# One table and one 8 KB gather for both expert vectors, in tiles of 64 tokens by 2 heads

## What is computed

```python
v1, i1 = lax.top_k(s1, TOPK_HALF)          # 128 key scores per half, the best 16
v2, i2 = lax.top_k(s2, TOPK_HALF)
cand_s = v1[..., :, None] + v2[..., None, :]   # 256 candidates per head
top_s, pos = lax.top_k(cand_s, TOPK)           # the best 16
gate = jax.nn.softmax(top_s, axis=-1)
u = expert_u[it]                               # (tokens, 8, 16, 1024)
vv = expert_v[it]
act = jax.nn.gelu(jnp.einsum('thkd,td->thk', u, xt), approximate=False)
return jnp.einsum('thk,thkd->td', gt * act, vv)
```

## Time and profile before

| | us |
|---|---|
| median of 3 runs | 3206.51 (3203.05 to 3211.17) |
| span of the profiled execution | 3215.5 |
| TensorE busy | 2267.0 (71%) |
| VectorE busy | 2051.6 (64%) |
| ScalarE busy | 296.6 (9%) |
| GpSimd busy | 2249.6 (70%) |
| moved | 1210.54 MB, mean 376 GB/s |

### The profile page before, as it was taken

How to read it: one execution, slowest core, us unless ns; L and a number is a source line. 1 busy time by engine, 2 the same in 40 slices (tenths; PEclk the granted TensorE clock), 3 DMA queues, 4 the chain that set the end, 5 groups by cost and what they waited for, 6 DMA issues and landing times.

```text
span 3215.5 us, 27380 instructions
## 1 busy us (share of the span) xinstructions
PE 2267.0 (71%) x9248; PEld 950.2 (30%) x9248; DVE 2051.6 (64%) x4962; ACT 296.6 (9%) x476; POOL 2249.6 (70%) x2062
## 2 busy tenths in 40 slices
PE   7877568878666588777765578887767665556666
PEld 5553323423233134223322224432322221111111
DVE  2588865666777855655788855666587776444441
ACT  1120001110000011111000000122000000000000
POOL 0246666787777776777777776778777777777775
PEclk9878779889778799989877788889988887787668
DMA  5799999999999999999999999999999999999998
GB/s 198 280 344 363 375 359 409 409 342 410 379 367 378 367 410 409 400 352 377 409 394 382 382 372 409 383 360 346 384 402 382 406 376 384 408 408 406 409 410 321
DMA packets 332348, 1210.54 MB, mean 376 GB/s; under 512 B 37040, under 2 KB 37168, under 8 KB 332208
## 3 DMA queue, kind: packets, MB, share of 16 engines
q0 software_dynamic: 294912, 1073.87, 86.5%
q1 hardware_dynamic: 37296, 134.91, 11.0%
HBM read 1204.44 MB, written 4.19 MB: 376 GB/s over the span
## 4 chain that ended last, share of the span: by engine, by line
POOL 35%; issue 12%; DVE 10%; DMA 7%; PE 6%; ACT 0%; POOLq 0%; DVEq 0%
POOL v_ring L436 18%; POOL u_ring L424 17%; DMA v_ring<-table_v,idx_v 5%; DVE u_ring L998 4%; DMA u_ring<-table_u,idx_u 3%; PE acc L632 2%; PE pt L462 2%; PE po L462 1%; DVE rc L867 1%; DVE rc L872 1%; DVE top_i L818 0%; DVE top_i L828 0%; DVE top_v L825 0%; DVE top_v L815 0%; DVE sum_p L853 0%
## 5 line engine op out<-in xcount | busy, mean ns | idle before, releaser
L998 DVE CUSTOM_DVE_ANT_0 u_ring<-u_ring,h2s 128x1024 f32<-128x1024 f32 x1024 | 1238.6, 1223 | 884.1 <-DMA u_ring<-table_u,idx_u 870.6
L632 PE MATMUL acc<-v_ring,wmask 128*32 128x512 f32 x4096 | 1229.4, 765 | 558.4 <-DMA v_ring<-table_v,idx_v 512.7
L424 POOL DMA_INDIRECT u_ring<-table_u,idx_u x1024 | 1115.4, 1089 | 604.5 <-issue 297.8
L436 POOL DMA_INDIRECT v_ring<-table_v,idx_v x1024 | 1130.5, 1104 | 349.4 <-issue 303.4
L632 PEld LDWEIGHTS acc<-v_ring,wmask 128*32 128x32 f32 x4096 | 220.7, 126 | 1435.9 <-DMA v_ring<-table_v,idx_v 1144.2
L462 PE MATMUL pt<-hT,w_ring 128*128 128x256 f32 (+1 forms) x1440 | 276.9, 350 | 10.5 <-DVE uT L911 9.9
L462 PEld LDWEIGHTS pt<-hT,w_ring 128*128 128x128 f32 x1440 | 237.1, 199 | 56.3 <-issue 32.8
L462 PE MATMUL po<-hT,w_ring 128*128 128x256 f32 (+1 forms) x800 | 158.2, 353 | 9.6 <-ACT kT L692 7.7
L462 PEld LDWEIGHTS po<-hT,w_ring 128*128 128x128 f32 x800 | 132.2, 198 | 38.7 <-issue 25.1
L618 PE MATMUL small<-ident,idx_f 128*32 128x32 f32 x256 | 13.5, 242 | 157.6 <-DVE idx_u L881 150.3
L451 PE MATMUL pt<-ident,rb 128*128 128x128 f32 x284 | 48.1, 321 | 68.2 <-ACT rb L667 42.2
(11 more groups left out here) (160 smaller groups left out, 1669.6 us busy)
## 6 DMA issues: line engine op xcount, KB each, us to landing
w_ring<-wstream SPq DMA_DIRECT2D x240, 512.0 KB, 6.8
u_ring<-table_u,idx_u POOLq DMA_INDIRECT x1024, 7.9
v_ring<-table_v,idx_v POOLq DMA_INDIRECT x1024, 7.9
xs<-x_in_dram SPq DMA_DIRECT2D x8, 512.0 KB, 8.3
y_out_dram<-xs SPq DMA_DIRECT2D x8, 512.0 KB, 6.6
g_all<-norm SPq DMA_DIRECT2D x1, 512.0 KB, 8.2
keysT<-keys SPq DMA_DIRECT2D x1, 128.0 KB, 7.2
chan_sb<-chan SPq DMA_DIRECT2D x1, 19.0 KB, 7.8
```

What stands on the lines that cost most here:

```text
L424: nc.gpsimd.indirect_dma_start(out=u_ring[:, k % U_SLOTS, :], out_offset=None, in_=peer_u, in_offset=bass.IndirectOffsetOnAxis(ap=idx_u[:, ...
L436: nc.gpsimd.indirect_dma_start(out=v_ring[:, slot, :], out_offset=None, in_=peer_v, in_offset=bass.IndirectOffsetOnAxis(ap=idx_v[:, b % ST ...
L632: mm = nc.tensor.matmul(acc[32 * i:32 * i + 32, half * 512:(half + 1) * 512], wmask[:, quarter % 2, i, 32 * j:32 * j + 32], v_ring[:, t % ...
L998: d = V.tensor_tensor_reduce(u, u, h2s[:, b % STASH, :], 1.0, 0.0, ALU.mult, ALU.add, dots[:, quarter % 2, at:at + 1])
```

## The change

The two tables become one, `table_uv`, with 2048 columns: a row holds an expert's U row and behind it its V row, so one gather of 128 rows of 8 KB (1 MB) brings both. For this the U and the V side must share one tile: tile `t` holds 64 tokens (half `t % 2` of a block) times the two heads of a quarter, at one pick rank. One ring of 8 slots of 8 KB replaces two rings of 8 slots of 4 KB. The diff, cut to its core:

```diff
-        u_ring = sb("u_ring", [P, U_SLOTS, D])
-        v_ring = sb("v_ring", [P, V_SLOTS, D])
+        ring = sb("ring", [P, SLOTS, 2 * D])
...
+        def place(t):
+            b, q, r, i = t // PICKS, t % PICKS // QPICKS, t % QPICKS // 2, t % 2
+            return b, q, i, r
...
-            for s in range(BLOCKS * GROUPS + V_LAG):
-                if s >= V_LAG:
-                    gather_v(s - V_LAG)
-                if s < BLOCKS * GROUPS:
-                    gather_u(s)
+            for t in range(TICKS):
+                b, q, i, r = place(t)
+                if t % QPICKS == 0:
+                    pool.wait_ge(idx_kept, picked(b, q))
+                if t % 2 == 0:
+                    wait(pool, pair_done, (t - SLOTS) // 2 + 1)
+                nc.gpsimd.indirect_dma_start(
+                    out=ring[:, t % SLOTS, :], out_offset=None, in_=table,
+                    in_offset=bass.IndirectOffsetOnAxis(ap=idx_t[:, b % STASH, q, i, r:r + 1], axis=0),
+                ).then_inc(uv_in[t % SLOTS], 16)
...
+            def mix(p):
+                if p % PAIRS == 0:
+                    wait(pe, acc_free, p // PAIRS)
+                pe.wait_ge(wmask_ready, p + 1)
+                for half in range(2):
+                    for i in range(2):
+                        slot = (2 * p + i) % SLOTS
+                        mm = nc.tensor.matmul(acc[HALF * i:HALF * i + HALF, half * 512:(half + 1) * 512],
+                                              wmask[:, slot, :],
+                                              ring[:, slot, D + half * 512:D + (half + 1) * 512],
+                                              start=(p % PAIRS == 0), stop=(p % PAIRS == PAIRS - 1))
+                mm.then_inc(pair_done, 1)
...
+                if k % 2 == 0 and 0 < k <= TICKS:
+                    mix(k // 2 - 1)
                 for step in STEPS.get(k, ()):
...
+            def gate_mask(p):
+                for t in (2 * p, 2 * p + 1):
+                    b, q, i, r = place(t)
+                    a = nc.scalar.activation(gmask[:, t % SLOTS, :], stack[:], copy,
+                                             scale=gate_t[:, b % STASH, q, i, r:r + 1])
+                a.then_inc(gmask_ready, 1)
+            def weigh(p):
+                lo = 2 * p % SLOTS
+                act.wait_ge(dots_done, p + 1)
+                nc.scalar.activation(acts[:, lo:lo + 2], dots[:, lo:lo + 2], ACT.Gelu).then_inc(gelu_done, 1)
+                act.wait_ge(gmask_ready, p + 1)
+                act.wait_ge(gelu_done, p + 1)
+                for slot in (lo, lo + 1):
+                    a = nc.scalar.activation(wmask[:, slot, :], gmask[:, slot, :], copy,
+                                             scale=acts[:, slot:slot + 1])
+                a.then_inc(wmask_ready, 1)
```

```diff
-        (566, 748, 780, 812, 844)]
+        (584, 744, 776, 808, 840)]
```

More of the change, by code:

```diff
@@ L125, in front_steps, with peer, ranks @@
     main += [(2.0, ("h2", b)) for b in blocks]
+    def peer(p):
+        return [(piece, ("w", PIECE_PEER + 4 * p + c)) for c in range(4)] + [(3.0, ("key_scores", p))]
+    def ranks(b, q):
+        return [(7.0, ("rank", b, q)), (5.5, ("combine", b, q)), (0.5, ("gate", b, q)),
+                (6.5, ("look_up", b, q)), (1.5, ("turn_picks", b, q))]
+    if f == 0:
+        first = ranks(0, 0)
+        main += peer(0) + first[:2] + peer(1) + peer(2) + first[2:4] + peer(3)[:2] + first[4:] + peer(3)[2:]
+        return [main] + [ranks(0, q) for q in range(1, 4)]
     sections = [main, [], [], []]
     for q, section in enumerate(sections):
-        for p in (range(0) if f == 0 and q else range(4) if f == 0 else (q,)):
-            main_or_own = main if f == 0 else section
-            main_or_own += [(piece, ("w", PIECE_PEER + 4 * p + c)) for c in range(4)]
-            main_or_own += [(3.0, ("key_scores", p))]
+        section += peer(q)
         for b in blocks:
-            section += [(9.0, ("rank", b, q)), (7.0, ("combine", b, q)), (8.0, ("look_up", b, q)),
-                        (3.0, ("turn_picks", b, q))]
-            section += [(2.0, ("gate", b, q)), (2.0, ("gate_norm", b, q))]
+            section += ranks(b, q)
     return sections
@@ L160, in picked, with build @@
     return 4 * FIRST[f] + q * SUPER[f] + (b - FIRST[f]) + 1
-def build(nc, x, wstream, chan, keys, norm2_g, peer_u, peer_v, out):
+def build(nc, x, wstream, chan, keys, norm2_g, table, out):
     with ExitStack() as ctx:
@@ L602, in front @@
                     small_bank("picks")
-                    spread_out(pick_cols, idx_f).then_inc(idx_turned, 1)
-            small_uses = {"picks": 0, "weights": 0, "sums": 0}
+                    for h in range(2):
+                        for half in range(2):
+                            mm = nc.tensor.matmul(small[HALF * h:HALF * h + HALF, 32 * half:32 * half + 32],
+                                                  ident[:, HALF * half:HALF * half + HALF], turn_src[:, h, :],
+                                                  start=True, stop=True)
@@ L607, in small_bank @@
+                    mm.then_inc(idx_turned, 1)
+            small_uses = {"picks": 0, "sums": 0}
             def small_bank(what):
                 wait(pe, idx_kept, small_uses["picks"])
-                wait(pe, wmask_ready, small_uses["weights"])
                 wait(pe, sum_kept, small_uses["sums"])
                 small_uses[what] += 1
-            def spread_out(dst, src):
-                every = ident[:].rearrange("p (c a) -> p a c", a=4)
-                for a in range(4):
-                    mm = nc.tensor.matmul(dst[32 * a:32 * a + 32, :], src[:], every[:, a, :], start=True, stop=True)
-                return mm
@@ L759, in _ @@
                 for step in STEPS.get(k, ()):
                     front(*step)
+                if k % 2 == 0 and 0 <= k < TICKS:
+                    gate_mask(k // 2)
         @block.vector
@@ L964, in front @@
                     dve.wait_ge(invh_ready, b + 1)
-                    step(V.scalar_tensor_tensor(h2s[:, b % STASH, :], xs[:, b % X_SLOTS, :], invh[:, i:i + 1],
-                                                g2_all[:], ALU.mult, ALU.mult))
+                    for half in range(2):
+                        r = slice(HALF * half, HALF * half + HALF)
+                        last = V.scalar_tensor_tensor(h2r[r, b % H_SLOTS, half, :], xs[r, b % X_SLOTS, :],
+                                                      invh[r, i:i + 1], g2_all[r, :], ALU.mult, ALU.mult)
+                        if half == 0:
+                            step(last)
+                    last.then_inc(h2_ready, 1)
                 if name == "rank":
@@ L1019, in finish @@
             def finish(b):
-                dve.wait_ge(group_done, (b + 1) * GROUPS)
+                dve.wait_ge(pair_done, (b + 1) * PAIRS)
                 row = xs[:, b % X_SLOTS, :]
```

216 lines of the change are left out of this document (72 added, 144 removed).

## The result

The changed kernel took 3651.61 us (median of 4 runs, 3648.68 to 3659.98), the kernel before 3208.84 us beside it (4 runs, 3203.05 to 3217.25): a ratio of 1.138, 95% interval 1.136 to 1.141. The forecast was 3103 us, and 3235 at most.

A forecast was written before the change was run, and what follows sets the result against it. The prediction took GpSimd's gather issue as the bound where VectorE disturbs it, DMA elsewhere. For the change, 127.5 + 2903 + 8.5 = 3039, plus 48 and 25, made 3112 us profiled, less 9: 3103 us, range 2985 to 3235.

The forecast's parts named there:

- What the edits put on the path: Chain from landing to free slots: single delays of 5 to 7 us absorbed; attention adds 48 us, convolution 25 us.
- in every stage: Sign of failure: the forecast fails if TensorE's waits for ScalarE's masks, expected in attention, stand in every stage.
- Gathers go by rows: GpSimd: a gather of 8 KB rows costs 1.39 us with its gap, as for 4 KB; 1423 us in all.
- DMA as the only limit: Whole kernel: first gather at 127.5, 1184.5 MB at 408 GB/s in 2903 us, tail 8.5; sum 3039 us.
- Rival (a): Whole kernel: stands absorbed, DMA full throughout, 3030 us or 2995; 8 KB rows could also move faster; chance 0.22.
- Mixing: TensorE: 64-column matmuls of neighbours overlap, 0.43 us each, 1.71 us a pair of tiles.
- rival (d): TensorE's mixing: 64-column matmuls don't overlap, 0.9 us more per tile, over 3300 us in all; chance 0.04.
- Chain of a pair: From last landing through dots, gelu, masks and matmuls 4.1 us, then 1.2 us for the gather's issue.
- Attention slot: Attention: TensorE's 9.0 us of work plus 3.5 us standing, 12.5 us against 11.3 of gathers; 40 slots, 48 us.
- Convolution group: Convolution, per channel group: 14.7 us of TensorE's work plus a 4.1 us stand, 18.8 against 16.7; 25 us for 12.
- ScalarE: Masks, gelus and table loads add 780 us to 297, a third of the span, delaying only through the chain.
- Rival (b): Whole kernel: TensorE stands behind ScalarE and VectorE, its clock falls to 0.75, 3260 us; threshold 0.39 us a tick; chance 0.17.

The follow-up runs named there:

- e13: Changed kernel with TensorE mixing by gate masks that need no dots; slots still wait for dots, gelu and masks: 3173.39 us, 0.987 of the kernel before.
- e1: Changed kernel without the mixing: one dummy product per block, slots freed when ScalarE's masks are ready: 3021.44 us, 0.892 of the kernel before.
- e17: Changed kernel with TensorE's mixing behind its front steps and one tick later, VectorE's dot ahead of its front steps: 3115.43 us, 0.969 of the kernel before.
- e7: Changed kernel with two gathers of 4 KB rows per tile from separate tables instead of one of 8 KB: 3681.03 us, 1.146 of the kernel before.

## Why the prediction was wrong

The step that failed is **"What the edits put on the path"**, in the sentence "A single delay of some 5 to 7 us on VectorE, ScalarE or TensorE is therefore absorbed" and in "Two kinds do", which priced all coupling at 48 + 25 = 73 us. It treated delays of the three engines as separate events against one slack. They are one loop: late masks delay a mixing, this delays TensorE's front steps, and they delay the front steps of ScalarE and VectorE, behind which the next gelu and the next dot stand. A turn costs the sum of its members: in the attention 7.8 us for a pair on average, 10.03 in the timeline shown first, against 5.14 of traffic. e13 cuts one edge of it and gets 480 us; the forecast was too low by 550. The prediction's own sign of failing, waits for masks "in every stage", is what came.

The loss isn't one of attention alone. Some 40 slots at 18.2 us in place of 12.5 are 230 us and 12 convolution groups at 20.2 in place of 18.8 are 17, an estimate from the windows below. The other 300 us lie in stages for which the sum had nothing. In ticks 744 to 840 only queries, key scores and ranking run beside the gathers, and "ranking costs nothing" stood for them: they take 299 us (dots at 2884 and 3183) where e1 takes 248 (2303 and 2551).

- **Gathers go by rows.** Right: 1091 ns and the 0.3 us gap, 1.39 us as forecast. The first gather stood at 129.1 us, forecast 127.5.
- **DMA as the only limit.** 3039 for an execution, and e1 took 3020.0, but in part by luck. The rate of the stretch alone is 422, not 408, with which the same sum gives 2943 (2807 for the 1184.5 MB); the other 77 us of e1 went in slices of 350 to 392 GB/s and a first gather at 136.6 us. 408 was read as what the DMA engines can do. But in that stretch GpSimd has no wait either (305.2 us busy and 94.7 between gathers, of 400), so its issue may as well have set the 408. Rival (a)'s remark on longer rows came true in the number; whether the row's length or GpSimd's spare time makes the 422 isn't shown. "DMA: Bandwidth & Descriptors" ("Specifications") of the Trainium skill has 435 GB/s as the ceiling, and no stretch shown here reaches it.
- **Mixing.** At full clock a pair took 1.94 us against 1.71, so rival (d) falls. In the mean it took 2.71 (1387.5 us for 512 pairs), because TensorE was often granted the lower level. By the rule of "TensorEngine Tiling (Array Packing)" ("Theoretical Speedup") of the Trainium skill, up to 4x at 32 columns, the mixing of before would have taken half of its 3.42 us, an estimate. The traces have about 2x at either width: four matmuls of 64 columns take 1.94 us and not the 3.52 of four whole ones, and the 32 columns of before did little better.
- **Chain of a pair.** 4.1 us after the landing, nearly right at full clock, as the stretch of gathers alone shows (dot at 3459.65, gather at 3464.07, 4.4 us), and 6.5 us with a mixing of 3.50 at the lower level (dot at 3464.60, gather at 3471.09):

```profile
3459.65 1.23 DVE L997 CUSTOM_DVE_ANT_0 ring<-ring,h2r 128x1024 f32<-128x1024 f32 x1 [1.25 <-DMA ring<-table_uv,idx_t]
...
3461.85 1.94 PE L614 MATMUL acc<-ring,wmask 128*64 128x512 f32 x8 [1.77 <-ACT wmask L743]
...
3464.07 0.94 POOL L431 DMA_INDIRECT ring<-table_uv,idx_t  x1 [1.15 <-PE acc L614]
3464.60 1.22 DVE L997 CUSTOM_DVE_ANT_0 ring<-ring,h2r 128x1024 f32<-128x1024 f32 x1 [1.25 <-DMA ring<-table_uv,idx_t]
...
3466.80 3.50 PE L614 MATMUL acc<-ring,wmask 128*64 128x512 f32 x8 [3.02 <-ACT wmask L743]
...
3471.09 0.94 POOL L431 DMA_INDIRECT ring<-table_uv,idx_t  x1 [4.45 <-PE acc L614]
```

  There eight slots do absorb the chain, at 422 GB/s. What they don't absorb is the front in the loop.
- **Attention slot, 12.5 us.** Measured 18.2. Of this TensorE is busy 12.0 (144.27 / 12) where 9.0 was taken, partly because its clock fell to 0.78, and idle 6.2 where 3.5 was taken. All of these 6.2 us are waits for masks (73.9 / 12): the stand behind the sigmoids, 4.2 to 5.8 us long, and a second one, mostly of 1.8 to 2.1 us and eight times in the twelve slots, behind the copy of the transposes, which the prediction didn't see. With the lag (e17) the slot takes 12.3. The rate was forecast near 370 GB/s and was 275.
- **Convolution group, 18.8 us.** Measured 20.2, from the first and the last of four groups; 17.2 in e17:

```profile
2372.65 0.43 DVE L913 TENSOR_TENSOR uT<-pt,conv_t 128x256 f32<-128x256 f32 x1 [12.93 <-PE pt L451]
...
2433.13 0.42 DVE L913 TENSOR_TENSOR uT<-pt,conv_t 128x256 f32<-128x256 f32 x1 [10.26 <-PE pt L451]
```

  VectorE's waits of 12.93 and 10.26 us for the product of a weight piece are VectorE's part of the loop, which the prediction saw ("TensorE's next mixing then waits for VectorE") and priced once, for this stage alone.
- **ScalarE.** 767 us more work where 780 was forecast. Its work is no bound, but the place of gelu in its queue is a member of the loop. Its two masks take 0.59 us and not 0.46. "ScalarE: Activation LUTs" ("What ACT_TABLE_LOAD costs") of the Trainium skill has 2.66 us for a switch, a drain included. Here a load takes 1.28 and no drain shows: in e17 a load starts at 2098.77, 0.02 us after the masks ahead of it end (2098.17 + 0.58), and gelu starts at 2100.07.
- **Rival (b)** had the direction and the engines, with a chance of 0.17 and 3260 us, 392 too low. It priced the lower clock (14.2 us a slot) and still one stand a slot. Its own threshold, 0.39 us a tick, was passed twofold: from block 0 to block 5 the changed kernel took 3.63 us a tick and e1 2.83.

## What to carry to other kernels

When two queues carry work of two kinds, and each has a step of one kind that waits for a step of the other kind in the other queue, follow the ring once round and add up its members; a buffer's slack doesn't cover a delay that comes back every turn. Put the consumer of a long chain (here the mixing) behind the independent work of its queue, by as many steps as the ring of buffers allows, and try the lag as a row: here 3652, 3280, 3135, 3131 us, and 3200 where a lag of three met an earlier dot. A merge that takes a buffer with a lag of its own away (here V's 36 ticks) takes the decoupling with it, and this belongs in the sum as much as the work saved.

## What the runs showed of the hardware

- Gathers of 8 KB rows alone run at 422 GB/s, while GpSimd waits for half of the time (151.5 of 300 us from 3300 on). Rows of 4 KB ran at 405 in the same structure (e7) and 408 in the kernel before, with GpSimd never waiting. So these rows don't part the row's length from GpSimd's issue.
- A gather of 128 rows costs GpSimd the same for 4 KB and 8 KB rows: mean 1.08 to 1.10 us in e7 and 1.09 in the changed kernel.
- TensorE's mixing ran at 1.94 us a pair and at 3.50 us in one stretch with the DMA engines full; the mean clock there was 0.74. In the attention too it took 1.94 and up to 3.68 us. Its clock was 0.78 over the twelve slots of the changed kernel, with 6.2 us of waits a slot, and 0.92 over the same work in e17.
- The lag of two with the dot first, which waits for its ring, took the same time within 0.1% beside a kernel before of 3366 us and one of 3218. The kernel before, whose GpSimd issues gathers nearly all the time, differed by 5% between sets. Nothing here shows what differs.
